# Two transformer layers with hierarchical experts: last projection half in two pieces, experts chosen by pair comparisons, ranks in bf16, gather handed over in halves

## The reference

```python
h = h + mixer(rms_norm(h, norm)) @ w_out
hf = rms_norm(h, m_norm)
g_logits = hf @ w_group + b_group                         # 4 groups
g_idx = argmax(g_logits); g_prob = softmax(g_logits)[g_idx]
e_logits = (hf @ w_router + b_router)[group g_idx]        # 8 experts of the group
top_val, top_idx = top_k(e_logits, 2)
weights = softmax(top_val) * g_prob
for e in range(32):                                       # FF = 256
    hid = silu(hf @ w_gate[e]) * (hf @ w_up[e])
    y += (hid @ w_down[e]) * combine[:, e]
h = h + y
```

## Time and profile before

| | us |
|---|---|
| median of 3 runs | 910.77 (910.54 to 917.93) |
| the profiled execution's own time | 910.19 |
| its span | 908.0 |
| PE busy | 787.3 (87%) |
| DVE busy | 323.2 (36%) |
| ACT busy | 200.2 (22%) |
| transfers | 242.03 MB, mean 267 GB/s |

### The profile page before, as it was taken

The page is one execution under the profiler, slowest core; times in us unless marked ns, Lnnn a source line. Parts: engine busy times, 40 slices in busy tenths (PEclk is TensorE's granted clock), DMA queues, the critical chain, the costliest instruction groups (busy, mean ns, idle before and its releaser), DMA issues.

```text
span 908.0 us, 16901 instructions
## 1 busy us (share of the span) xinstructions
PE 787.3 (87%) x7574; PEld 524.9 (58%) x7574; DVE 323.2 (36%) x682; ACT 200.2 (22%) x391; POOL 12.9 (1%) x62
## 2 busy tenths in 40 slices
PE   8999799698999997889988999997998967668766
PEld 6778677684565554645554778886455534334422
DVE  4563755532163224143323305543044222112212
ACT  3562245420230000000003043352040000000002
POOL 5000000000000000000000000000000000000000
PEclk9999899998999999999999999999999998889889
DMA  9442001308739999999999633005846999999993
GB/s 270 142 110 95 1 2 40 150 3 330 288 129 414 421 420 421 421 366 422 422 419 370 225 125 107 34 1 192 364 185 253 422 421 421 419 421 420 420 422 154
DMA packets 61091, 242.03 MB, mean 267 GB/s; under 512 B 9414, under 2 KB 33084, under 8 KB 36060
## 3 DMA queue, kind: packets, MB, share of 16 engines
q1 hardware_dynamic: 60956, 240.94, 67.3%
q10 hardware_dynamic: 64, 0.02, 0.0%
HBM read 239.90 MB, written 1.05 MB: 265 GB/s over the span
## 4 chain that ended last, share of the span: by engine, by line
PE 64%; DMA 23%; DVE 6%; ACT 3%; issue 2%; SPq 1%; PEldq 0%; POOL 0%; DVEq 0%; POOLq 0%
DMA M<-in_m_w_down_dram 11%; PE ps L1294 10%; PE ps L814 9%; PE ps L1117 8%; PE ps L1011 6%; DMA M<-in_m_w_gate_dram 6%; DMA M<-in_m_w_up_dram 6%; PE ps L1081 5%; PE ps L1157 4%; PE ps L1094 3%; PE ps L962 2%; PE ps L928 1%; DVE H L1732 1%; PE ps L897 1%; PE ps L1023 1%
## 5 line engine op out<-in xcount | busy, mean ns | idle before, releaser
L1117 PE MATMUL ps<-M 128*32 128x256 f32 x2048 | 129.1, 408 | 41.0 <-DMA M<-in_m_w_gate_dram 31.9
L1117 PEld LDWEIGHTS ps<-M 128*32 128x32 f32 x2048 | 73.3, 117 | 106.5 <-issue 65.1
L1294 PE MATMUL ps<-M 128*128 128x256 f32 (+2 forms) x400 | 92.8, 390 | 1.0 <-DVE M L1419 1.0
L814 PE MATMUL ps<-M 128*128 128x272 f32 x352 | 89.0, 407 | 1.0 <-DVE M L1419 1.0
L1081 PE MATMUL ps<-M 128*128 128x128 f32 x688 | 81.9, 279 | 3.7 <-DVE M L1797 3.7
L1294 PEld LDWEIGHTS ps<-M 128*128 128x128 f32 (+1 forms) x400 | 73.6, 187 | 17.1 <-issue 4.7
L1081 PEld LDWEIGHTS ps<-M 128*128 128x128 f32 x688 | 80.0, 195 | 5.5 <-DVE M L1797 4.6
L1157 PE MATMUL ps<-M 128*32 128x512 f32 x512 | 67.2, 610 | 14.5 <-DMA M<-in_m_w_down_dram 9.2
L1729 DVE TENSOR_TENSOR H<-H,ps 128x512 f32<-128x512 f32 x68 | 46.7, 687 | 89.6 <-PE ps L1094 89.3
L1094 PE MATMUL ps<-M 128*128 128x512 f32 x136 | 68.3, 623 | 9.9 <-DVE H L1732 6.8
L814 PEld LDWEIGHTS ps<-M 128*128 128x128 f32 x352 | 67.1, 195 | 16.4 <-issue 2.0
(11 more groups left out here) (346 smaller groups left out, 829.8 us busy)
## 6 DMA issues: line engine op xcount, KB each, us to landing
M<-in_m_w_gate_dram SPq DMA_DIRECT2D x32, 2048.0 KB, 18.9
M<-in_m_w_up_dram SPq DMA_DIRECT2D x32, 2048.0 KB, 23.6
M<-in_m_w_down_dram SPq DMA_DIRECT2D x32, 2048.0 KB, 25.9
M<-in_o_w_in_dram SPq DMA_DIRECT2D x12, 1024.0 KB, 5.6
M<-in_e_w_in_dram SPq DMA_DIRECT2D x11, 1024.0 KB, 5.2
M<-in_e_w_out_dram SPq DMA_DIRECT2D x1, 4096.0 KB, 14.1
M<-in_o_w_out_dram SPq DMA_DIRECT2D x1, 4096.0 KB, 18.6
H<-in_x_dram SPq DMA_DIRECT2D x2, 512.0 KB, 4.1
```

The source lines that it names most:

```text
L814: ins = pe.matmul(ps[:, n % 4, 0:T], wringE[:, (n // 2) % 4, k, (n % 2) * P:(n % 2) * P + P], xnE[:, k], start=(k == 0), stop=(k == KD - 1))
L1117: ins = pe.matmul(ps[32 * e:32 * e + 32, 3 * x, 0:FF], xgT[q % 2][:, k, 32 * e:32 * e + 32], gu_w[UNIT_SLOT[y][u]][:, e, k, :], start=(k = ...
L1294: ins = pe.matmul(ps[rows, unit % 4, 0:n], lhs(k), rhs(k), start=(k == 0), stop=(k == KD - 1))
```

## The change

Five edits. **1.** The last 512-column half of the projection of tile 1 becomes two sums of 256 columns, the second itself split over its eight steps; transposes and logit products of tile 1 stand between the pieces. `h_res` and `res_done` count one more per layer, and SP's wait at `u == 3` moves with them. ACT squares tile 1 in two pieces, and scales tile 0 between them. **2.** The two experts come from comparing the eight logits pair by pair: for expert i, `rk` - i + 7 is the number of experts ahead of it; `A8` marks the two with none or one ahead, `oh1` the one with none. **3.** `AA`, the triangle and the ones of the rank products are bf16; ranks and counts have a semaphore count each, and counts are read later; `RM` is now rank + 1 or 0, compared with integers from 1 on. **4.** The weights are worked out behind the first gather's scaling, `onehot` and the weighted copy are apart, and the overflow table moves from quad 0 to quad 1. **5.** Each half of the gather (and of its scaling) has a count of its own, and the gate products wait at `k == 0` and `k == 4`. The filler products go from 4 + 2 to 3 + 1.

```diff
@@ SP, experts
-                        sp.wait_ge(s("res_done"), 5 if y == 0 else 9)
+                        sp.wait_ge(s("res_done"), 6 if y == 0 else 11)
@@ ACT, experts
-                act.wait_ge(s("h_res"), h0 + 5 - y)
-                root(1 + 2 * y, 1, junkM)
-                warm_up(ACT.Exp)
...
+                act.wait_ge(s("h_res"), h0 + 5 - y)
+                link(nc.scalar.activation(junkM[:, 1, 0:768], H[:, 1, 0:768], ACT.Square, accum_out=ss[:, ri, 1:2]))
+                link(nc.scalar.activation(ss[:, ri, 1:2], ss[:, ri, 1:2], ACT.Identity, bias=epsb[:, 0:1], scale=1.0 / D))
+                act.wait_ge(s("rec"), (5, 10)[y])
+                normed(0)
+                act.wait_ge(s("h_res"), h0 + 6 - y)
+                link(nc.scalar.activation(junkM[:, 1, 768:D], H[:, 1, 768:D], ACT.Square, accum_out=ss[:, ri, 3:4]))
+                nc.scalar.activation(rs[:, ri, 1:2], ss[:, ri, 3:4], ACT.Sqrt, bias=ss[:, ri, 1:2], scale=1.0 / D) \
+                    .then_inc(s("sqr"), 1)
                 act.wait_ge(s("rec"), (6, 11)[y])
-                normed(0)
+                normed(1)
+                if nt == 3:
+                    normed(2)
+                warm_up(ACT.Exp)
                 act.wait_ge(s("route_in"), 2 * y + 1)
                 nc.scalar.activation(eg[:, 0:nt], eg[:, 0:nt], ACT.Exp).then_inc(s("route_exp"), 1)
-                normed(1)
...
-                if nt == 3:
-                    normed(2)
@@ PE, out_proj
-                half(1, 1)
+                part(1, 512, 256, 3)
                 pe.wait_ge(s("h_res"), h0 + 4 - y)
                 turned(1, range(0, 4), 7)
...
                 ins = logits(0)
                 if y == 0:
                     pe.wait_ge(s("hr_act"), 2)
                     ins = logits(2)
                 ins.then_inc(s("lg_done"), 1)
+                part(1, 768, 256, 0, range(0, 4))
                 pe.wait_ge(s("h_res"), h0 + 5 - y)
-                turned(1, range(4, 8), 0)
+                turned(1, range(4, 6), 5)
                 pe.wait_ge(s("hr_act"), (3, 5)[y])
-                pe.wait_ge(s("hr_dve"), 2 + 2 * y)
-                logits(1).then_inc(s("lg_done"), 1)
-                keep_busy(4, 6)
+                logits(1, range(0, 4))
+                part(1, 768, 256, 0, range(4, 8))
+                pe.wait_ge(s("hr_dve"), 2 + 3 * y)
+                logits(1, range(4, 6))
+                pe.wait_ge(s("h_res"), h0 + 6 - y)
+                turned(1, range(6, 8), 6)
+                pe.wait_ge(s("hr_dve"), 3 + 3 * y)
+                logits(1, range(6, 8)).then_inc(s("lg_done"), 1)
+                keep_busy(3, 1)
@@ PE, experts
-                terms = [[(before, 0)], [(ones, 0), (before, 1)]]
+                terms = [[(before_h, 0)], [(ones_h, 0), (before_h, 1)]]
...
+                ins.then_inc(s("rk_done"), 1)
                 for x in range(nt):
                     c = TILES[x][1]
-                    ins = pe.matmul(ps[:, 7, 96:96 + NE], ones[0:c, :], AA[0:c, x], start=(x == 0), stop=(x == nt - 1))
+                    ins = pe.matmul(ps[:, 6, 0:NE], ones_h[0:c, :], AA[0:c, x], start=(x == 0), stop=(x == nt - 1))
                 ins.then_inc(s("rk_done"), 1)
-                keep_busy(2, 6)
-
-                def gather():
+                keep_busy(1, 1)
+
+                def gather(done=None):
...
+                        if done is not None and k == 3:
+                            ins.then_inc(done, 1)
...
                 def half_gu(u, q, x):
                     for k in range(KD):
+                        if x == 0 and k % 4 == 0:
+                            pe.wait_ge(s("xg_set"), 2 * (NQ * y + q) + k // 4 + 1)
@@ DVE, set-up, ahead of the chunk masks
+            eight = iota[:, 0:8]
+            tt(low[:, :, :], eight.unsqueeze(1).to_broadcast([P, 8, 8]), eight.unsqueeze(2).to_broadcast([P, 8, 8]), ALU.is_lt)
+            v.tensor_scalar(rkc[:, 0], eight, -6.0, None, ALU.add)
+            v.tensor_scalar(rkc[:, 1], eight, -7.0, None, ALU.add)
+            v.tensor_copy(ones_h[:, :], ones[:, :])
+            v.tensor_copy(before_h[:, :], before[:, :])
@@ DVE, experts
-                res_add(5 - y, 1, 1)
+                res_add(5 - y, 1, 512, 256, 3)
+                logit(0)
+                if y == 0:
+                    logit(2)
                 v.wait_ge(s("hr_tr"), h0 + 5 - y)
-                v.tensor_copy(hrT[:, 4:8, TOK[1]], ps[:, 0, :].rearrange("p (k t) -> p k t", k=4)).then_inc(s("hr_dve"), 1)
+                v.tensor_copy(hrT[:, 4:6, TOK[1]], ps[:, 5, 0:256].rearrange("p (k t) -> p k t", k=2)).then_inc(s("hr_dve"), 1)
+                res_add(6 - y, 1, 768, 256, 0)
+                v.wait_ge(s("hr_tr"), h0 + 6 - y)
+                v.tensor_copy(hrT[:, 6:8, TOK[1]], ps[:, 6, 256:512].rearrange("p (k t) -> p k t", k=2)).then_inc(s("hr_dve"), 1)
                 invert(ri, 1)
...
+                logit(1)
...
-                link(v.tensor_reduce(v1[:, t_], el[:, t_], AXX, ALU.max))
-                first_max(oh1, el[:, t_], v1, 8, s8)
-                link(stt(out=el[:, t_], in0=oh1[:, t_], scalar=-3e38, in1=el[:, t_], op0=ALU.mult, op1=ALU.add))
-                link(v.tensor_reduce(v2[:, t_], el[:, t_], AXX, ALU.max))
-                tt(w2[:, t_], v2[:, t_], v1[:, t_], ALU.subtract).then_inc(s("route_in"), 1)
-                first_max(oh2, el[:, t_], v2, 8, s8)
-                tt(O1[:, t_], inner(oh1), groups(ohg), ALU.mult)
-                link(tt(O2[:, t_], inner(oh2), groups(ohg), ALU.mult))
...
-                tt(AA[:, t_], f1, f2, ALU.add).then_inc(s("A_set"), 1)
...
+                link(tt(GE[:, t_], el[:, t_].unsqueeze(2).to_broadcast([P, nt, 8, 8]), el[:, t_].unsqueeze(3).to_broadcast([P, nt, 8, 8]),
+                        ALU.is_ge))
+                link(tt(GE[:, t_], GE[:, t_], low[:, :, :].unsqueeze(1).to_broadcast([P, nt, 8, 8]), ALU.mult))
+                link(tt(DF[:, t_], GE[:, t_], GE[:, t_].rearrange("p t b a -> p t a b"), ALU.subtract))
+                link(v.tensor_reduce(rk[:, t_], DF[:, t_], AXX, ALU.add))
+                link(tt(A8[:, t_], rk[:, t_], row(rkc[:, 0]), ALU.is_le))
+                tt(by_group(AA), inner(A8), groups(ohg), ALU.mult).then_inc(s("A_set"), 1)
+                tt(eg[:, t_], top, wide3(gmax, NG), ALU.subtract).then_inc(s("route_in"), 1)
+                v.tensor_reduce(v1[:, t_], el[:, t_], AXX, ALU.max)
+                link(tt(oh1[:, t_], rk[:, t_], row(rkc[:, 1]), ALU.is_equal))
...
-                v.wait_ge(s("rk_done"), y + 1)
-                v.tensor_copy(cnts, ps[:, 7, 96:128])
+                v.wait_ge(s("rk_done"), 2 * y + 1)
                 link(stt(out=RM[:, t_], in0=ps[:, 7, 0:32 * nt].rearrange("p (t e) -> p t e", t=nt), scalar=1.0, in1=AA[:, t_],
                          op0=ALU.add, op1=ALU.mult))
-                link(v.tensor_scalar(RM[:, t_], RM[:, t_], -1.0, None, ALU.add))
...
+                def gathered_set(q):
                     for b in range(2):
...
+                        v.wait_ge(s("g_done"), 2 * (NQ * y + q) + b + 1)
+                        gathered(q, b).then_inc(s("xg_set"), 1)
...
                 onehot(0)
-                v.wait_ge(s("g_done"), NQ * y + 1)
-                gathered(0).then_inc(s("xg_set"), 1)
+                second_logit()
+                gathered_set(0)
+                weights()
+                weighted(0)
                 for q in range(NQ):
...
                         onehot(q + 1)
-                    if q == 0:
+                        weighted(q + 1)
+                    if q == 1:
```

More of the change, by code:

```diff
@@ L1007, in out_proj, with part @@
                     ins.then_inc(s("res_done"), 1)
[L1009 to L1013, removed]
+                def part(n, c0, w, bank, ks=range(8)):
+                    for k in ks:
+                        ins = pe.matmul(ps[:, bank, 0:w], mixT[:, k, TOK[n]], wo[:, k, c0:c0 + w], start=(k == 0), stop=(k == 7))
+                    if ks[-1] == 7:
+                        ins.then_inc(s("res_done"), 1)
                 def turned(n, ks, bank):
@@ L1018, in turned, with logits @@
                     ins.then_inc(s("hr_tr"), 1)
-                def logits(n):
+                def logits(n, ks=range(KD)):
                     cnt = TILES[n][1]
-                    for k in range(KD):
+                    for k in ks:
                         ins = pe.matmul(ps[0:cnt, 2 if n == 1 else 4, n * 36:n * 36 + 36], hrT[:, k, TOK[n]], wrc[:, k, :],
@@ L1619, in experts, with res_add, logit @@
                 link(v.memset(LG, 0.0))
-                def res_add(m, n, hf):
+                def res_add(m, n, c0, w, bank):
                     v.wait_ge(s("res_done"), h0 + m)
-                    c = slice(512 * hf, 512 * hf + 512)
-                    tt(H[:, n, c], H[:, n, c], ps[:, 2 * n + hf, :], ALU.add).then_inc(s("h_res"), 1)
+                    c = slice(c0, c0 + w)
+                    tt(H[:, n, c], H[:, n, c], ps[:, bank, 0:w], ALU.add).then_inc(s("h_res"), 1)
```

(29 more changed lines are left out.)

100 lines of the change are left out of this document (45 added, 55 removed).

## The result

The changed kernel took 904.05 us in the median of 11 runs (901.01 to 906.47), the kernel before 913.87 us in runs beside it. The ratio is 0.9888 with a 95% interval of 0.9863 to 0.9913: faster by 1.1%, some 10 us, where 9.2 were forecast (0.990). The profiled execution took 902.73 us, 7.5 less than the one of before.

The account below looks back on a forecast made before the run. Each expert stage hangs on the end of the first gate product. Choice 1.2 and 1.3, ranks to gather 2.55 and 1.6, gather halves 1.35 twice, less 0.15, made 9.2 us: 901.6 us, range 899.8 to 906.2.

Parts of the forecast that it names:

- the prediction's own signs of being wrong: Clock 0.50 in the gather, tile 1's logits a microsecond off, or the end moving less than the fifth units.
- rival (a): TensorE's clock at 0.50 falls on gather or gate: 903.1 us for one layer, 904.6 for both; chance 0.20.
- What bounds it: Expert stages, stream and products alike, hang on the first gate product's end; each layer loses what the serial piece ahead loses.
- its 265.7: Time in us at which the first layer's fifth unit of expert weights was forecast to be issued.
- Projection and logits, gain 0: From tile 1's last projection product to its logits: 13.40 us forecast against 13.33, so no gain.
- the 0.6: Allowance in us, either way per layer, for miscounted overlap in projection and logits.
- Choice, 1.2 and 1.3: Choosing the two experts on VectorE, up to the first rank product: 1.2 and 1.3 us gained in layers 1 and 2.
- bf16 at 0.10: Price in us of one narrow bf16 rank or count product, taken between 0.057 and 0.13.
- The filler at 0.99: One filler product between counts and gather in the first layer, priced at 0.99 us.
- Halves, 1.35: Gather handed over in halves so that scaling is hidden: 1.35 us gained in each layer.
- Moved work at nothing: Set-up operations, ScalarE's last scaled tile, weights' chain and overflow table fall into idle or covered time, at no cost.
- Sum, 9.2: Total saving over both layers, 9.2 us, giving 901.6 us on the median of 910.77.

Follow-up runs that it names:

- experiments 2 to 4: The changed kernel with, in turn, the old choice of experts (0.9941), ranks and counts in fp32 (0.9933), the gather handed over whole (0.991); ratios to the kernel before.
- experiment 6: The changed kernel with five fillers ahead of the ranks and none between counts and gather, instead of three and one: 903.99 us, ratio 0.9893 to the kernel before.
- experiment 4: The changed kernel with the gather handed over whole, the gate waiting once for both scalings: 908.03 us, ratio 0.991 to the kernel before.
- experiment 2: The changed kernel with the old choice of the two experts, bf16 ranks and all else kept: 909.15 us, ratio 0.9941 to the kernel before.

## Why the prediction was right, and where not

The measured 904.05 us lies in the stated range of 899.8 to 906.2, but above the part of it that was given 0.60, which ends at 903, and one of the prediction's own signs of being wrong came true: the granted clock was 0.50 in the first layer's gather. In the two stretches the result is the forecast's sum with rival (a) in one layer.

*What bounds it*, right: the full stretches moved as blocks, the fifth units went 4.98 and 6.84 us earlier, and the end 6.9, and experiments 2 to 4 lost in the time what the stretches lost, as far as their intervals tell. That the first fifth unit met its 265.7 so closely (265.83) is luck: 1.50 of its 4.98 us came from the mixer ahead.

*Projection and logits, gain 0*: right, 13.44 against 13.40 in the first layer; the 0.3 us gained in the second, inside the 0.6, are the logits at full clock, not overlap.

*Choice, 1.2 and 1.3*: 1.06 and 1.22. The open price was the 8 x 8 block read in turned order: 0.50 us at 192 elements for 0.36 of an operation of that size read straight, 0.14 of the 0.4 that I had left open. The Trainium skill (SBUF — State Buffer, Door 1: The DMA port swizzle) has a penalty for each access that crosses to a new 16-byte line; the row points the same way, and nothing here tests it.

*bf16 at 0.10*: too dear. Six products start within 0.22 us (253.36 to 253.58), and all nine (six for the ranks, three for the counts) fill the 0.60 us from 253.36 to the filler at 253.96, where 0.90 were counted; in the second layer five take 0.14 us for 0.50. The lower end, 0.057 each, was the better row: 0.51 and 0.29. The Trainium skill (TensorE: Matmul & The Clock Gate, Weight-path perf modes) has a faster weight load for 128 weights not in fp32. The trace goes the same way, at the 0.3 us a layer that was named: most of these records start 0.02 to 0.04 us apart, the fp32 ones of the kernel before 0.11. But a product in fp32 is also two records for one, and no run parts the two.

*The filler at 0.99*: in the first layer 1.50, partly under the half clock; this and the gather's 6.83 for 5.52 are rival (a), one layer of it, priced at 1.5 us and worth 1.6 (30.12 less the 28.51 of experiment 6). It held in every kernel that had three fillers and one, the pieces and the pairs (first-layer gather 6.8 to 7.0 us). I gave it 0.20, too little: the argument against it, that the gather is dense and that a fall would come in the fillers, failed, because the clock fell behind the idle piece, at about 254.7, and the gather's first 2.7 us ran under it. I counted fillers and left out where they stand.

*Halves, 1.35*: right, 1.5 in each layer by experiment 4. *Moved work at nothing*: right for set-up, table and weights; ScalarE's last tile ended at 252.7 instead of 254.6 and never mattered.

*Sum, 9.2*: 8.15 in the two stretches, 9.8 between the medians of 11 runs, 6.7 from the 910.77 that the forecast started from. That the second is the closer is luck: the kernel before ran slower in its later runs, and outside the stretches 1.50 were gained and 2.8 lost in the profiled pair.

## What to carry over

A chain of small operations between two dense stretches of TensorE has two prices: its own time, and the granted clock that its idle piece can cost the dense stretch behind it. So a step in it can be worth more than its length (0.88 us of chain cost 2.45 in experiment 2) or just its length (0.66 us cost 0.64 in the other layer, where a spell was there anyway). Before taking fillers out or moving a step, read the windows at the start of the next dense stretch, not the number of fillers. Put the fillers where the idle time is (here all ahead of the ranks), and let them end before the work behind them is ready: in the overflow turn three of them ended 0.7 us too late.

## What was not expected of the hardware

An idle piece of 1.66 us, with small products around it, came ahead of a spell at 1.2 GHz in every kernel that had it (gather 6.83 us for 5.52 in the changed one). One of 1.2 us did not in the five kernels with bf16 ranks (gather 3.81 us), but did with fp32 ranks behind it (4.74). Nine bf16 products of 32 columns with new weights each took 0.60 us from the first one's start to the filler; the same nine in fp32, eighteen records, took 2.5 at full clock in the kernel before (255.81 to 258.27).
